# Wider steps in a dense layer, its last products by token block, and output parts ahead of the last attention heads

## What is computed

```python
def swiglu(h, w_gate, w_up, w_down):
    return (jax.nn.silu(h @ w_gate) * (h @ w_up)) @ w_down

def reference(x, norm_g, pool_w, ...):
    for i in range(DEPTH):
        h = rms_norm(x, norm_g[i, 0])
        if i % N_MIXERS == 0:
            y = pool_mixer(h, pool_w[slot], pool_scale[slot])
        else:
            y = forgetting_attention(h, attn_w_in[slot], attn_b_f[slot], attn_w_out[slot])
        x = x + rms_norm(y, norm_g[i, 1])
        h = rms_norm(x, norm_g[i, 2])
        if i % N_MIXERS == 0:
            y = swiglu(h, ffn_w_gate[slot], ffn_w_up[slot], ffn_w_down[slot])
        else:
            y = moe_swiglu(h, w_router, w_gate, w_up, w_down)
        x = x + rms_norm(y, norm_g[i, 3])
```

## Time and profile before

| | before |
|---|---|
| median of three runs | 1280.48 us |
| profiled execution, its own time | 1283.84 us |
| its span on the core | 1281.9 us |
| PE busy | 1224.0 us (95%) |
| DVE, ACT busy | 698.7 us, 542.9 us |
| HBM read | 412.5 MB, 323 GB/s over the span |

### The profile page before, as it was taken

One profiled execution on the slowest core, in us unless ns is written; L12 is line 12 of the kernel. 1 busy time (PEld: TensorE's weight loads), 2 busy tenths in 40 slices (PEclk: granted clock), 3 DMA queues, 4 the chain that ended last, 5 costly groups with the idle time before them and its releaser, 6 DMA issues.

```text
span 1281.9 us, 17304 instructions
## 1 busy us (share of the span) xinstructions
PE 1224.0 (95%) x6616; PEld 886.0 (69%) x6616; DVE 698.7 (55%) x781; ACT 542.9 (42%) x516; POOL 105.3 (8%) x119
## 2 busy tenths in 40 slices
PE   8899999889999999999899999989999989999996
PEld 8799999778878788633588853468883347888332
DVE  5754544656657889400598920078871026887102
ACT  4434343355535677300577710067760025775001
POOL 0000000000001222010005001000501000050100
PEclk9899999999999999999999999999999998999999
DMA  9955656453336899999999999999999999999995
GB/s 301 321 195 168 195 166 195 127 165 104 129 120 235 326 373 366 337 401 402 409 409 404 407 409 409 402 409 409 402 409 409 403 407 409 409 402 381 399 402 216
DMA packets 151065, 414.67 MB, mean 323 GB/s; under 512 B 8704, under 2 KB 48640, under 8 KB 150912
## 3 DMA queue, kind: packets, MB, share of 16 engines
q1 hardware_dynamic: 150032, 409.79, 84.6%
q0 software_dynamic: 960, 3.80, 0.9%
HBM read 412.52 MB, written 1.05 MB: 323 GB/s over the span
## 4 chain that ended last, share of the span: by engine, by line
PE 85%; DMA 5%; DVE 4%; issue 2%; SPq 2%; ACT 2%; DVEq 0%; ACTq 0%
PE bank L1229 20%; PE bank L1230 19%; PE bank L1231 19%; PE bank L1516 14%; DMA raw<-in_moe_w_gate 4%; PE bank L1529 4%; SPq L473 1%; PE bank L1469 1%; PE bank L1592 1%; DVE raw_lo L789 1%; PE bank L1546 1%; ACT w_hi L532 1%; DMA raw<-in_pool_w 1%; PE bank L1236 1%; PE bank L1414 1%
## 5 line engine op out<-in xcount | busy, mean ns | idle before, releaser
L789 DVE TENSOR_TENSOR raw_lo<-raw,w_hi 128x2048 fp32r<-128x2048 f32 x170 | 388.4, 2299 | 142.8 <-ACT w_hi L532 142.6
L532 ACT ACTIVATE w_hi<-raw 128x2048 fp32r<-128x2048 f32 x170 | 325.2, 1916 | 225.2 <-PE bank L1231 160.3
L1229 PE MATMUL bank<-w_hi,h_hi 128*128 128x512 f32 (+1 forms) x848 | 301.6, 356 | 30.8 <-DVE h_lo L1084 10.2
L1231 PE MATMUL bank<-w_hi,h_lo 128*128 128x512 f32 (+1 forms) x848 | 296.8, 350 | 0.0
L1230 PE MATMUL bank<-raw_lo,h_hi 128*128 128x512 f32 (+1 forms) x784 | 272.1, 347 | 0.0
L1229 PEld LDWEIGHTS bank<-w_hi,h_hi 128*128 128x128 f32 x848 | 165.0, 195 | 59.9 <-DVE raw_lo L789 22.6
L1231 PEld LDWEIGHTS bank<-w_hi,h_lo 128*128 128x128 f32 x848 | 165.1, 195 | 20.4
L1230 PEld LDWEIGHTS bank<-raw_lo,h_hi 128*128 128x128 f32 x784 | 153.0, 195 | 16.7
L1516 PE MATMUL bank<-raw,h_b 128*64 128x512 f32 (+1 forms) x768 | 143.3, 523 | 0.8 <-DMA raw<-in_moe_w_up 0.7
L1229 PE MATMUL bank<-w_hi,aT_hi 128*128 128x512 f32 x312 | 123.9, 397 | 1.5 <-DVE aT_lo L925 1.5
L1231 PE MATMUL bank<-w_hi,aT_lo 128*128 128x512 f32 x312 | 121.7, 390 | 0.0
(11 more groups left out here) (240 smaller groups left out, 1283.7 us busy)
## 6 DMA issues: line engine op xcount, KB each, us to landing
raw<-in_moe_w_gate SPq DMA_DIRECT2D x96, 1024.0 KB, 15.9
raw<-in_moe_w_up SPq DMA_DIRECT2D x80, 1024.0 KB, 16.1
raw<-in_moe_w_down SPq DMA_DIRECT2D x64, 1024.0 KB, 14.3
raw_extra<-in_moe_w_down SPq DMA_DIRECT2D x48, 1024.0 KB, 16.2
raw_extra<-in_moe_w_up SPq DMA_DIRECT2D x32, 1024.0 KB, 13.5
raw_extra<-in_moe_w_gate SPq DMA_DIRECT2D x16, 1024.0 KB, 14.2
raw<-in_ffn_w_gate SPq DMA_DIRECT2D x11, 1024.0 KB, 5.4
raw<-in_ffn_w_up SPq DMA_DIRECT2D x11, 1024.0 KB, 5.3
```

The source lines that it names most:

```text
L532: nc.scalar.activation(w_hi[:, slot, :], raw_slot(source), ACT.Copy).then_inc(hi_ready, 1)
L789: nc.vector.tensor_tensor(lo_slot(source), raw_slot(source), w_hi[:, slot, :].bitcast(f32), ALU.subtract).then_inc(lo_ready, 1)
L1229: mm(out, a_hi, b_hi, start=first, stop=False)
L1231: return mm(out, a_lo, b_hi, start=False, stop=last)
```

## The change

It has four parts.

1. **Dense layer in wider steps.** One step of 256 hidden columns as before, then five of 512. A wide step has two gate, two up and two down units. Gate products go to banks 0 and 1 and up products to banks 2 and 3, one bank for each token block, with 512 columns a matmul. Each block's activation has its own tiles (`silu_w`, `act_w`, `aT_hi_w`, `aT_lo_w` for block 1) and its own four transposes, block 0's between the two gate units, block 1's behind them. There are six places for high parts in this stage: three more lie where `head_row`, `qk` to `pT`, and `v` will be.
2. **Last step by token block.** The down products of the last two steps are ordered so that block 0 is complete first (24 matmuls, then 24), then block 1 (48 matmuls). Block 0's transposes for the values stand inside the last of these. The 30 filler matmuls are gone.
3. **Values and forget gates by block.** Three of the four value units run for block 0 ahead of the transposes of block 1, and the forget gates are made for each block: 48 matmuls of 128 columns in place of 24 of 256. The load of `head_row` now waits until value unit 36 is used, since that tile's room holds a high part until then.
4. **Output parts ahead.** Three of the eight output parts (the first for both blocks, the second for block 0) stand ahead of the last pair's transposes and outputs. Part (3, 0), which completes block 0, is now followed by two parts and not by three.

```diff
-            for g in range(N_FG):
-                if g < N_FG - 1:
-                    pe.wait_ge(silu_done, g + 1)
-                    ffn_in(u_gate(g + 1), bank[0])
-
-                transpose_act(g + 1, [act[:, tb * FG + f * P:tb * FG + (f + 1) * P] for f in range(2) for tb in range(TB)])
-                if g < N_FG - 1:
-                    ffn_in(u_up(g + 1), bank[1])
-                pe.wait_ge(aT_lo_done, g + 1)
...
+            def ffn_wide(u, i, banks, free):
+
+                hi, lo = weights(u + i, HALF)
                 for tb in range(TB):
+                    tok = slice(tb * P, (tb + 1) * P)
+                    if i == 0 and free[tb] is not None:
+                        pe.wait_ge(*free[tb])
+                    for k in range(4):
+                        kb = 4 * i + k
+                        step = three(banks[tb][:, :], h_hi[:, kb, tok], h_lo[:, kb, tok], hi[:, k, :], lo[:, k, :],
+                                     kb == 0, kb == KB - 1)
+                step.then_inc(unit_used, 1)
...
+            for s in range(LAST_FS):
+                gate_free = [(silu_done, at_f(s, tb)) for tb in range(TB)] if s > 0 else [(silu_done, 1), (act_done, 1)]
+                up_free = [(aT_lo_done, at_f(s, tb)) for tb in range(TB)] if s > 0 else [(aT_lo_done, 1), None]
+                ffn_wide(u_gate(s + 1), 0, bank[0:2], gate_free)
+                act_transposed(s, 0)
+                ffn_wide(u_gate(s + 1), 1, bank[0:2], None)
+                if s > 0:
+                    act_transposed(s, 1)
+                for i in range(2):
+                    ffn_wide(u_up(s + 1), i, bank[2:4], up_free)
+                if s < LAST_FS - 1:
+                    pe.wait_ge(aT_lo_done, at_f(s, 1))
+                    for i in range(units_f(s)):
+                        ffn_down(s, i, range(TB))
+            s = LAST_FS - 1
+            pe.wait_ge(aT_lo_done, at_f(s, 1))
+            ffn_down(s, 0, [0])
+            act_transposed(LAST_FS, 0)
+            ffn_down(s, 1, [0]).then_inc(down_half, 1)
+            act_transposed(LAST_FS, 1)
+            pe.wait_ge(aT_lo_done, at_f(LAST_FS, 0))
+            ffn_down(LAST_FS, 0, [0])
+            ffn_down(LAST_FS, 1, [0]).then_inc(y0_psum, 1)
+            ffn_down(s, 0, [1])
+            ffn_down(s, 1, [1])
+            pe.wait_ge(aT_lo_done, at_f(LAST_FS, 1))
+            ffn_down(LAST_FS, 0, [1])
+            ffn_down(LAST_FS, 1, [1], lambda: input_transposed(2, 0))
...
-            keep_warm(WARM[1])
-            for tb in range(TB):
-                input_transposed(2, tb)
+            pe.wait_ge(small_lo, 2)
+            for tb in range(TB):
+                if tb == 1:
+                    input_transposed(2, 1)
+                pe.wait_ge(h_lo_done, 2 * 4 + 2 * tb + 1)
+                v_unit(0, [tb])
                 pe.wait_ge(h_lo_done, 2 * 4 + 2 * tb + 2)
-                v_unit(0, [tb])
                 v_unit(1, [tb])
-            pe.wait_ge(small_lo, 2)
-            three_t(bank[2][0:H, 0:T], wf2, H).then_inc(f_psum, 1)
-            v_unit(2)
+                step = forget(tb)
+                v_unit(2, [tb])
+            step.then_inc(f_psum, 1)
             v_unit(3)
...
+            pe.wait_ge(o_lo_done, 4)
+            out_part(0, 0)
+            out_part(1, 0)
+            pe.wait_ge(mx_done, H)
+            out_part(0, 1)
+            heads_transposed(H // 2 - 1)
+            head_outputs(H // 2 - 1)
+            out_part(2, 0)
+            out_part(1, 1)
+            pe.wait_ge(o_lo_done, H // 2)
+            out_part(3, 0)
+            out_part(2, 1)
+            out_part(3, 1)
```

ACT and DVE in the dense layer follow the same steps; the high parts' places, and the order of ACT:

```diff
+        def hi_place(u):
+
+            if u >= QK_U0:
+                return u % SPLIT_SLOTS
+            if u < 3:
+                return (3, 1, 2)[u]
+            return (1, 5, 3, 4, 2, 0)[(u + 2) % 6]
...
+            def aT_high_dense(s, tb):
+                sc.wait_ge(aT_psum, at_f(s, tb))
+                if s == LAST_FS:
+                    sc.wait_ge(down_half, 1)
+                elif s > 0:
+                    sc.wait_ge(unit_used, u_down(s - 1) + units_f(s - 1))
+                nc.scalar.activation(aT_dense(s, tb)[0][:, :], bank[2 + tb][:, :], ACT.Copy).then_inc(aT_hi_done, 1)
...
+            for s in range(LAST_FS):
+                g = u_gate(s + 1)
+                hi_upto(g + 4)
+                aT_high_dense(s, 0)
+                hi_upto(g + 5)
+                if s > 0:
+                    aT_high_dense(s, 1)
+                for tb in range(TB):
+                    silu_dense(s + 1, tb)
+                hi_upto(g + 7)
+            hi_upto(V_U0 + 1)
+            for tb in range(TB):
+                aT_high_dense(LAST_FS, tb)
...
             post_squares(3, 0, ffn_out, (y0_psum, 2), in_xn, after=3)
-            post_squares(3, 1, ffn_out, (unit_used, V_U0), in_xn)
+            hi_upto(V_U0 + 2)
             squares(4, 0)
-
+            hi_upto(V_U0 + 3)
             input_hi(2, [0])
+            post_squares(3, 1, ffn_out, (unit_used, V_U0), in_xn, after=5)
             squares(4, 1)
+            hi_upto(QK_U0)
             input_hi(2, [1])
-            hi(V_U0 + 2)
-            hi(V_U0 + 3)
-            hi(QK_U0)
...
-                if n == 2:
-
-                    po.wait_ge(y_done, 4)
+                if n == 4:
+
+                    po.wait_ge(unit_used, V_U0 + 3)
                     po.dma_start(head_row[:, :, :], heads_d.bitcast(f32r)).then_inc(heads_in, 16)
```

257 lines of the change are left out of this document (153 added, 104 removed).

## The result

The changed kernel takes 1272.72 us (median of 4 runs: 1269.86, 1272.21, 1273.22, 1273.70); the kernel before, beside it, 1280.37. Ratio 0.9929, 95% interval 0.9915 to 0.9944. Measured again in 5 rounds among the experiments: 1270.64 us, ratio 0.9926 (0.9912 to 0.9940). So it is 0.7% faster, 7.7 to 9.5 us. The forecast was 1262.1 with a range of 1259 to 1268: right in sign, wrong in size by 10.6 us. One execution of all those behind this document, the seventh of before_placed, is left out of its ratio: it took 1374.19 us at a mean granted clock of 0.848, where the other ten of that kernel took 1279.49 to 1283.89.

The account below looks back on a forecast made before the run. PE's own pace bounds the dense layer, the weight stream the experts. Dense layer 7.0, turn 8.7 and output projection 2.65 sum to 18.35 us: 1280.48 - 18.35 = 1262.1 us, range 1259 to 1268.

Parts of the forecast that it names:

- Dense layer, 7.0 us won: Dense layer: 480 wide matmuls at 0.2278 us replace 960 narrow ones, 6.5 us; 0.4 and 0.1 at its end.
- rival 2: Dense layer: a wide product takes twice a narrow one, 240 ns, so 6.5 becomes 0: 1268.6 us; chance 0.02.
- Turn, 8.7 us won: Turn from dense layer to queries: 40.1 us becomes 31.4; 1.7 of the gain is the clock.
- I take 5 to 6, hidden: `head_row` load at the turn: lands in 5 to 6 us, hidden behind 5.47 us of PE work and 1.2.
- a wait on `head_row` at the queries: Start of the queries: listed among the profile signs that would show the forecast wrong.
- the forget gates: Turn: 24 matmuls of 128 columns at 115 ns, 2.75 us a block; bounds 1.4 to 5.35 us.
- The new order leaves no wait of that length: Turn: no wait long enough to halve the clock, so 2.4 GHz is counted on; 1.7 us of the gain.
- The 1.7 us that the forecast took back from the clock: Turn: 24 value products at 2.4 GHz take 5.47 us in place of 7.19 at half clock.
- Output projection, 2.65 us: Attention's end: moved parts win 5.6 us, 2.95 given back behind block 0's norm chain, so 2.65.
- All that is won arrives: Ahead of the experts: slots are full before the first expert product, so each microsecond won counts in full.
- Rival 1: Turn: gates 2 x 2.6 us dearer, `head_row` 1.9, or half clock 1.7; up to 1270.9, two of three 1267; chance 0.15.
- Rivals 3 and 4: 3: nine dense-layer handoffs each one split late, 38 us, 1300, chance 0.03. 4: expert stream fixes end, 1280.5, chance 0.02.

Follow-up runs that it names:

- before_placed: Kernel before the change, attention overlay and four extra expert slots moved to start 128 bytes past a multiple of 256: 1281.48 us, ratio 1.0009.
- late_all_256: Changed kernel with the `head_row` wait moved behind 48 products, every load slot, operand and overlay tensor starting on a multiple of 256 bytes: 1249.89 us, ratio 0.9745.

## Why the forecast was wrong, step by step

- *Dense layer, 7.0 us won.* Mis-sized: 4.0. The step "480 wide ones, 480 x 0.2278" took the pitch of products whose operands lay alike and used it for all. The change's new tensors start 32 bytes off the operands they meet, so of the layer's gate, up and down products, taken together, half ran at 232 to 234 ns. The trace of before could have warned, though none of its rows above shows it: the output projection's products, which read `o_lo`, ran at 233 ns, and the expert products with the extra slots at 231. Placed alike, the layer wins 6.4. So the fold itself wins nearly what was forecast; rival 2 (no gain) fell. That the layer began 0.6 us earlier came on top.
- *End of the layer.* Wait of 1.04, forecast 1.3: right.
- *Turn, 8.7 us won.* It won 6.7 (234.70 to 267.30 and 0.87, so 33.5 against 40.1). The step that failed is "I take 5 to 6, hidden": `head_row` took 9.8 us, so the queries came 3.6 us later than the value copies allow. The prediction had named a wait on `head_row` at the queries as a sign of being wrong. The row that priced it was at hand: 8.4 us beside a full stream, and I took a lower value because one load seemed little company. The wait of the first packet, about 4 us after the issue, is the same in both cases. Against that the forget gates were priced too dear: 24 take 1.4 us (0.06 each, the low end of my bounds), or 1.66 to the start of the next product, and not 2.75. With the wait moved the turn takes 29.9 us (234.21 to 263.21 and 0.87), 10.3 won.
- *The clock.* "The new order leaves no wait of that length" failed as the result of the wait on `head_row`: 2.7 us in the first head pair, and 1.4 at the router in the profiled execution. The first is shown by the fillers, and by the moved wait. The 1.7 us that the forecast took back from the clock behind the values' wait stand in the trace of before alone. In the four other traces of that kernel with padding the same wait lasts 1.89 to 1.98 us, and the 5.4 us and more behind it show 1.00, where before shows 0.71 (248.15 to 254). So those 1.7 us, taken from the median, may not have been there to win in most executions.
- *Output projection, 2.65 us.* Near in the number, less so in its terms. Undoing it cost 2.8, and the 2.95 given back behind it were 2.9 with the wait moved. But the projection took 24.85 us and not 23.9: its products read `o_lo`, at about 233 ns, before as after, and the forecast counted 227.8. In the kernel before, the stretch from 353.90 to 358.74 ran at a granted clock of 0.65, which the forecast left out. From before to the kernel with the wait moved this stage wins 1.7 in the traces, and in the changed kernel only 0.4, with the router at half clock.
- *All that is won arrives.* Right for the front: 9.1 us there, 10.5 at the end. In the expert stage itself the products are only part of the bound: 0.6 us with 400 products at a better pitch, 4.4 with faster loads, in one trace each.
- *Rivals.* Rival 1 had the right mechanism for half of the loss (`head_row` at 8.4, the clock once more) with gates that went the other way; at 1267 to 1270.9 it was nearest, and I gave it 0.15. (Any two of its three terms, 5.2, 1.9 and 1.7, give 1265.7 to 1269.2, not one number.) It priced the transfer at 1.9 and missed that the wait would drop the clock by itself. Rivals 3 and 4 did not come: no step waits for a split. Not one rival was about places, and they made 0.4%, about 5 us.

The sum from the changed kernel back to the forecast: 0.9926 to 0.9929 as measured, 0.5% for wait and clock, 0.4% for places, gives 0.9835, 1261.4 us, where 1262.1 was forecast. That the remainder is so small is in part luck. The cheap forget gates cancel against the clock's 1.7 us and the slower output products, and the places won back include those of `o_lo` and the extra slots, which the kernel before has as well. Open are how SyncE's loads hold up the first packet of `head_row`, and where 2 of the 5 us of the places were won. With all places alike one slower group is left: behind the transposes, products of the dense layer come every 230.9 ns in the mean. These are the 58 beside which ScalarE or VectorE reads a bank (late_all_256, 67 to 207 us, the first behind the transposes left out); the other 525 come every 226.7. No run moved those reads.

## What to carry to other kernels

A transfer that loses its slack is to be priced at its slowest row, with the clock that falls behind the wait added to it, and the wait put at the first instruction that reads the data. When a change adds tensors, look at where they start: give operands that meet in a product of 512 columns the same place within 256 bytes, and let the slots of a heavy load stream start on a multiple of 256. A shift of everything by 128 bytes, 0.8% here, is as large as many a reordering, so a change that moves allocations is to be tested against one that only pads.

## What the runs showed of the hardware

- The pitch of fp32r products depends on the relative starts of their operands in the partition: in the dense layer, 512 columns 226.7 ns alike modulo 256 bytes, 228.9 to 233.4 in the mean of a unit otherwise; 256 columns the other way, 119.9 alike and 117.8 with the weights 32 bytes off. Shifting both leaves it as it was.
- Loads into slots that start on a multiple of 256 bytes mostly ran at 413 to 421 GB/s in the expert stage, into slots 128 bytes off at 401 to 409; that was worth 0.8% of this kernel.
- With the starts alike, products beside which ScalarE or VectorE read a bank came every 230.9 ns, all others every 226.7.
- A GpSimd load of 640 KB took 9.7 us beside SyncE's loads, with or without two more behind it in its own queue. Its first packet started about 4 us after the issue; where SyncE's queue moved nothing, that of a 512 KB load started after 1.2.
- A product of 128 columns with 16 stationary came every 0.06 us.
